# One layer of an attention, recurrence and ConvGLU step: the tail folded into the last pair, and three stages reordered

## The reference

```python
h = rmsnorm(x, g_mix) * (1 + sc1) + sh1
q = (rmsnorm(pq, g_q) @ w_uq).reshape(B, T, 8, 96)      # 64 plain + 32 rotated columns
kv = (ckv_keys @ w_ukv).reshape(B, K, 8, 128)
o_mla = mla_attention(...)                              # 8 heads
o_hg = hgrn2_branch(...)                                # 4 heads
mix = sigmoid(ga) * (o_mla @ w_mla_o) + sigmoid(gb) * (o_hg @ w_hg_o)
x = x + gt1 * (mix @ w_out)
h2 = rmsnorm(x, g_ffn) * (1 + sc2) + sh2
gate, val = split(h2 @ w_ffn_in)
u = gelu(conv3(gate)) * val
x = x + gt2 * (u @ w_ffn_out)
y = rmsnorm(x, g_final)
```

## Time and profile before

| | us |
|---|---|
| three runs | 2227.31, 2230.32, 2235.73 (median 2230.32) |
| the profiled execution, its own time | 2230.21 |
| its span, first to last instruction | 2228.4 |
| TensorE busy | 2112.3 (95%) |
| VectorE busy | 964.8 (43%) |
| GpSimd busy | 785.8 (35%) |
| ScalarE busy | 652.1 (29%) |

### The profile page before, as it was taken

One profiled execution on the slowest core, in us unless ns is written; L12 is line 12 of the kernel. 1 busy time (PEld: TensorE's weight loads), 2 busy tenths in 40 slices (PEclk: granted clock), 3 DMA queues, 4 the chain that ended last, 5 costly groups with the idle time before them and its releaser, 6 DMA issues. The chain is left out here.

```text
span 2228.4 us, 28073 instructions
## 1 busy us (share of the span) xinstructions
PE 2112.3 (95%) x11544; PEld 1944.9 (87%) x11544; DVE 964.8 (43%) x1380; ACT 652.1 (29%) x939; POOL 785.8 (35%) x512
## 2 busy tenths in 40 slices
PE   7499999999999998999989889999999999999995
PEld 2479999999999988788879878999999999999994
DVE  2613535343414217556634357243334333433348
ACT  1333232323213334677652211311211121112120
POOL 0334353525213413445534622422322232223234
PEclk9599999999999999999999999999999999999998
DMA  6355311112221247233347423111111111111113
GB/s 239 113 186 112 41 53 32 53 32 60 63 70 48 90 122 211 73 86 85 87 136 203 156 76 104 57 40 37 57 39 38 39 56 40 39 38 53 43 67 132
DMA packets 191407, 183.96 MB, mean 83 GB/s; under 512 B 55047, under 2 KB 159200, under 8 KB 191280
## 3 DMA queue, kind: packets, MB, share of 16 engines
q1 hardware_dynamic: 189984, 177.44, 26.9%
q0 software_dynamic: 1296, 4.72, 0.6%
HBM read 141.36 MB, written 40.78 MB: 82 GB/s over the span
## 5 line engine op out<-in xcount | busy, mean ns | idle before, releaser
L129 POOL TENSOR_TENSOR s_w_lo<-s_w_raw,s_w_hi 128x1024 fp32r<-128x1024 f32 x86 | 219.9, 2557 | 512.4 <-ACT s_w_hi L124 512.4
L822 PE MATMUL s_psum<-h_hi,s_w_hi 128*128 128x384 f32 x1008 | 345.4, 346 | 24.8 <-POOL h_lo L250 24.8
L2567 PE MATMUL s_ps<-h_hi,s_w_hi 128*128 128x384 f32 x1056 | 353.1, 334 | 0.7 <-ACT gate_pad L2410 0.7
L2567 PE MATMUL s_ps<-h_hi,s_w_lo 128*128 128x384 f32 x1056 | 352.9, 334 | 0.0
L2567 PE MATMUL s_ps<-h_lo,s_w_hi 128*128 128x384 f32 x1056 | 352.8, 334 | 0.0
L822 PE MATMUL s_psum<-h_lo,s_w_hi 128*128 128x384 f32 x1008 | 338.8, 339 | 0.0
L822 PE MATMUL s_psum<-h_hi,s_w_lo 128*128 128x384 f32 x1008 | 338.5, 339 | 0.0
L822 PEld LDWEIGHTS s_psum<-h_hi,s_w_hi 128*128 128x128 f32 x1008 | 191.1, 190 | 34.9 <-issue 19.3
L2567 PEld LDWEIGHTS s_ps<-h_hi,s_w_hi 128*128 128x128 f32 x1056 | 198.2, 188 | 1.4 <-issue 1.0
L2567 PEld LDWEIGHTS s_ps<-h_lo,s_w_hi 128*128 128x128 f32 x1056 | 198.2, 188 | 0.4
L2567 PEld LDWEIGHTS s_ps<-h_hi,s_w_lo 128*128 128x128 f32 x1056 | 198.2, 188 | 0.0
(11 more groups left out here) (365 smaller groups left out, 3848.8 us busy)
## 6 DMA issues: line engine op xcount, KB each, us to landing
s_w_raw<-in_w_ffn_in SPq DMA_DIRECT2D x44, 512.0 KB, 3.7
s_w_raw<-in_w_in SPq DMA_DIRECT2D x41, 512.0 KB, 3.9
s_w_mod<-in_w_mod SPq DMA_DIRECT2D x8, 2048.0 KB, 8.0
w_raw<-in_w_ffn_out SPq DMA_DIRECT2D x11, 1024.0 KB
scratch_gates<-sig SPq DMA_DIRECT2D x48, 192.0 KB, 1.9
merge_gates<-scratch_gates SPq DMA_DIRECT2D x16, 576.0 KB, 3.9
w_mod<-in_w_mod SPq DMA_DIRECT2D x4, 2048.0 KB, 10.4
scratch_o_mla<-o_raw SPq DMA_DIRECT2D x8, 576.0 KB, 4.6
```

What stands on the lines that cost most here:

```text
L129: pool.tensor_tensor(flat[0], flat[1], flat[2], ALU.subtract).then_inc(self.lo_ready, 1)
L822: return pe.matmul(bank(j), wx[c % 2][:, k, :], hx[:, k, j * CH:(j + 1) * CH], start=(k == 0 and n == 0), stop=(k == KD - 1 and n == 2))
L2567: mm = pe.matmul(ps[bank][:, 0:CH], a[s][:, k, :], b[:, k, j * CH:(j + 1) * CH], start=n == 0, stop=n == 3 * KD - 1)
```

## The change

Four places are edited.

1. Attention units: the first head's three query units stand between value units 6 and 7 instead of behind the second k group. H and G of the first head stand behind unit k(1,2) instead of q(2,2), and its tops start behind q(1,0), one for each unit, instead of behind k(2,0). The F sums stand later.
2. Merge: blocks 2 and 3 of the attention rows are divided and split at later chunks (divided at 1, 2, 4, 6, split at 2, 3, 5, 7).
3. Out stage: tile t's transposes stand one by one behind outputs 6, 7, 8, 9, 11, 13, 15 and 17; DVE and ACT follow that order.
4. Tail: `yacc` is multiplied by gt2 (`z_gate`, nine of 128x1024 on DVE) and x1 is added to it (`z_add`, 18 of 128x512 on POOL) ahead of the end, in pairs 9 and 10, tile 8 first. What is left for a tile at the end is: both PSUM halves times gt2, one add of `yacc`, a square and sum that is on ACT now, the root, the reciprocal and the scale. TensorE's order there is the same; its banks are freed by the product with gt2 (`e_gated`) instead of by the sum (`e_sum`). gt2 is loaded twice more, x1 in 18 half rows through four buffers, and `gate_pad`, `conv` and `w2_raw` lie at other addresses to make room.

```diff
-    units = [("k", 0, u) for u in range(3)] + [("v", t, 0) for t in range(10)]
+    units = [("k", 0, u) for u in range(3)] + [("v", t, 0) for t in range(7)]
+    units += [("q", 0, u) for u in range(3)] + [("v", t, 0) for t in range(7, 10)]
     units += [("k", 1, u) for u in range(3)]
-    for h in range(HEADS):
+    for h in range(1, HEADS):
...
+FIRST_TOPS = {unit: n for n, unit in enumerate(B_UNITS[B_AT["q", 1, 0]:][:len(TOP_UNITS)])}
+FIXED_AFTER = {("q", 1, 0): 0, ("q", 1, 1): 1, ("q", 1, 2): 2, ("q", 2, 0): 3, ("q", 2, 1): 4}
...
-                if (kind, x, u) == ("q", 2, 2):
+                if (kind, x, u) == ("k", 1, 2):
                     item("H", 0, 0)
                     item("G", 0, 0)
...
+        X_DIV_AT, X_HI_AT, X_LO_AT = (1, 2, 4, 6), (2, 3, 5, 7), (2, 3, 5, 7)
...
-                    if c - 2 < KB:
-                        split_x(c - 2)
+                    if c in X_HI_AT:
+                        split_x(X_HI_AT.index(c))
...
-                    for ready in {3: (0,), 4: (1, 2), 5: (3,), 6: (4,), 7: (5, 6), 8: (7,)}[t]:
-                        transposes(ready)
+                        if o in TRANSPOSED_AFTER:
+                            transposes(TRANSPOSED_AFTER.index(o))
...
+                    if g == LAST - 1:
+                        sp.dma_start(gt2_once[:, :], io["rows"][3:4, :].to_broadcast([P, D])).then_inc(once_loaded, 16)
+                        for i in range(4):
+                            load_back(i)
...
+                for i in range(4, O_UNITS):
+                    load_back(i)
...
+                    act.wait_ge(e_x2, t + 1)
+                    if t >= 3:
+                        act.wait_ge(e_stored[t % 3], 16 * (t // 3))
+                    act.activation(fin[t % 3][:, :], x2[t % 3][:, :], ACT.Square, accum_out=stat[:, 3, t:t + 1]).then_inc(e_sq, 1)
...
+                def z_add(n):
+                    pool.wait_ge(z_gated, n + 1)
+                    for i in (2 * n, 2 * n + 1):
+                        cols = slice(i % 2 * HALF, (i % 2 + 1) * HALF)
+                        pool.wait_ge(back_loaded[i % 4], 16 * (i // 4 + 1))
+                        z = yacc[:, Z_TILES[n], cols]
+                        pool.tensor_tensor(z, z, x1_back[i % 4][:, :], ALU.add).then_inc(z_ready, 1)
...
+                z_add(0)
+                z_add(1)
+                w.split_lo(pool, 0, 4 * LAST + 2)
+                for t in range(2, 5):
+                    z_add(t)
+                w.split_lo(pool, 1, 4 * LAST + 3)
+                z_add(5)
+                z_add(6)
+                u_split(LAST, 0)
+                w2_split(LAST)
+                u_split(LAST, 1)
+                z_add(7)
+                z_add(8)
-                for t in range(TILES):
-                    pool.wait_ge(e_gated, t + 1)
-                    pool.wait_ge(back_loaded[t % 3], 16 * (t // 3 + 1))
-                    pool.tensor_tensor(x2[t % 3][:, :], yacc[:, t, :], x1_back[t % 3][:, :], ALU.add).then_inc(e_x2, 1)
...
-                        pe.wait_ge(e_sum, o - 7)
+                        pe.wait_ge(e_gated, o - 7)
...
+                    if g == LAST - 1:
+                        z_gate(0)
+                    if g == LAST:
+                        for n in range(5, TILES):
+                            z_gate(n)
                     conv_gate(g, 1)
                     value(g, 0)
                     value(g, 1)
+                    if g == LAST - 1:
+                        for n in range(1, 5):
+                            z_gate(n)
...
-                        dve.tensor_tensor(dst, dst, ps[(6 + o) % 8][:, :], ALU.add).then_inc(e_sum, 1)
-                    dve.wait_ge(e_sum, 2 * t + 2)
-                    dve.tensor_tensor(yacc[:, t, :], yacc[:, t, :], gt2[group(t)][:, :], ALU.mult).then_inc(e_gated, 1)
+                        dve.tensor_tensor(x2[t % 3][:, cols], ps[(6 + o) % 8][:, :], gt2[group(t)][:, cols], ALU.mult).then_inc(e_gated, 1)
...
-                    dve.tensor_tensor_reduce(fin[t % 3][:, :], x2[t % 3][:, :], x2[t % 3][:, :], 1.0, 0.0,
-                                             ALU.mult, ALU.add, stat[:, 3, t:t + 1]).then_inc(e_sq, 1)
...
                 for t in range(TILES):
-                    end_sums(t)
+                    end_gate(t)
+                    dve.wait_ge(e_gated, 2 * t + 2)
+                    dve.wait_ge(z_ready, O_UNITS)
+                    dve.tensor_tensor(x2[t % 3][:, :], x2[t % 3][:, :], yacc[:, t, :], ALU.add).then_inc(e_x2, 1)
                     if t >= 1:
-                        end_square(t - 1)
                         end_scale(t - 1)
```

More of the change, by code:

```diff
@@ L1371 @@
 TOP_UNITS = tuple(("M", u) for u in range(16)) + (("P", 0), ("P", 1), ("C", 0), ("T", 0))
-def first_tops():
-    out, n = {}, 0
-    for unit in B_UNITS[B_AT["k", 2, 0]:]:
-        take = 2 if unit[0] == "k" and unit[1] == 3 and unit[2] < 2 else 1
-        if n < len(TOP_UNITS):
-            out[unit] = range(n, min(n + take, len(TOP_UNITS)))
-        n += take
-    return out
-FIRST_TOPS = first_tops()
-FIXED_AFTER = {("q", 0, 1): (0,), ("q", 0, 2): (1,), ("q", 1, 0): (2,), ("q", 1, 1): (3,), ("q", 1, 2): (4,)}
+FIRST_TOPS = {unit: n for n, unit in enumerate(B_UNITS[B_AT["q", 1, 0]:][:len(TOP_UNITS)])}
+FIXED_AFTER = {("q", 1, 0): 0, ("q", 1, 1): 1, ("q", 1, 2): 2, ("q", 2, 0): 3, ("q", 2, 1): 4}
 HEAD_ITEMS = (
@@ L1598, in walk @@
                 unit(kind, x, u)
-                for n in FIXED_AFTER.get((kind, x, u), ()):
-                    item("F", n, 0)
+                if (kind, x, u) in FIXED_AFTER:
+                    item("F", FIXED_AFTER[kind, x, u], 0)
                 if (kind, x, u) == ("q", 0, 2):
@@ L2210 @@
 O_UNITS = 2 * TILES
+TRANSPOSED_AFTER = (6, 7, 8, 9, 11, 13, 15, 17)
 def flat_pieces(j):
@@ L2253, in stage_out_ffn @@
         yacc = late("yacc", [P, TILES, D])
-        over = Arena(nc, home.top)
+        over = Arena(nc, first.at)
         g_base = over.at
@@ L2258, in stage_out_ffn @@
         w2_raw = over("w2_raw", [P, 2, D])
-        assert over.at <= HIGH
+        gt2_once = over("gt2_once", [P, D])
+        x1_back = [over("x1_back3", [P, HALF])]
+        assert over.at <= HIGH - 8
         w2_hi, w2_lo = late("w2_hi", [P, 2, D], F32R), late("w2_lo", [P, 2, D], F32R)
         u_hi, u_lo = late("u_hi", [P, 2, NT], F32R), late("u_lo", [P, 2, NT], F32R)
+        x1_back = [late(f"x1_back{i}", [P, HALF]) for i in range(3)] + x1_back
         assert late.at <= first_end
@@ L2277, in stage_out_ffn @@
         gfin = end("g_final_row", [P, D])
-        x1_back = [end(f"x1_back{i}", [P, D]) for i in range(3)]
         x2 = [end(f"x2_{i}", [P, D]) for i in range(3)]
@@ L2295, in stage_out_ffn @@
         y_ps, y_added = sems("y_product"), sems("y_added")
-        end_rows, back_loaded = sems("end_rows"), [sems(f"back_loaded{i}") for i in range(3)]
-        e_ps, e_sum, e_gated, e_x2 = sems("end_product"), sems("end_sum"), sems("end_gated"), sems("end_x2")
+        end_rows, once_loaded, back_loaded = sems("end_rows"), sems("once_loaded"), [sems(f"back_loaded{i}") for i in range(4)]
+        z_gated, z_ready = sems("z_gated"), sems("z_ready")
+        e_ps, e_gated, e_x2 = sems("end_product"), sems("end_gated"), sems("end_x2")
         e_sq, e_std, e_rstd = sems("end_sq"), sems("end_std"), sems("end_rstd")
@@ L2306, in stage_out_ffn @@
         Y_PAIRS = PAIRS - 2
+        Z_TILES = (TILES - 1,) + tuple(range(TILES - 1))
         with nc.Block() as block:
@@ L2330, in load_w2, with load_back @@
                     sp.dma_start(w2_raw[:, :, :], wout[:, 2 * g:2 * g + 2, :]).then_inc(w2_loaded, 16)
+                def load_back(i):
+                    t, half = Z_TILES[i // 2], i % 2
+                    if i >= 4:
+                        sp.wait_ge(z_ready, i - 3)
+                    sp.dma_start(x1_back[i % 4][:, :], io["x1"][t * P:(t + 1) * P, half * HALF:(half + 1) * HALF]
+                                 ).then_inc(back_loaded[i % 4], 16)
                 load_wo(4)
@@ L2440, in _ @@
                 std(1)
-                std(2)
                 h_split(0)
-                std(3)
-                h_split(1)
-                h_split(2)
-                for t in range(4, TILES):
+                for t in range(2, TILES):
                     std(t)
@@ L2520, in _ @@
                 w.split_lo(pool, 0, 2)
-                for g in range(PAIRS):
+                def z_add(n):
[5 more added lines that the diff above has]
+                        pool.tensor_tensor(z, z, x1_back[i % 4][:, :], ALU.add).then_inc(z_ready, 1)
+                for g in range(LAST):
                     if g > 0:
@@ L2746, in _ @@
                 residual(1)
-                residual(2)
                 affine(0)
-                residual(3)
-                affine(1)
-                affine(2)
-                for t in range(4, TILES):
+                for t in range(2, TILES):
                     residual(t)
```

69 lines of the change are left out of this document (30 added, 39 removed).

## The result

| | before | changed |
|---|---|---|
| runs shown with the result, median | 2229.82 us (2227.31 to 2235.73) | 2198.72 us (2197.92 to 2200.13) |
| the profiled execution, its own time | 2230.21 | 2197.92 |
| its span | 2228.4 | 2196.1 |

The ratio is 0.985, with a 95% interval of 0.9835 to 0.9864 (the two medians of the table alone give 0.986): 31.1 us less by the medians, 32.3 by the two profiled executions. A second set of runs of the changed kernel gave 2198.58 (ratio 0.9853, 0.9839 to 0.9866). The forecast was 2205.6, 24.6 less, with a range of 2196 to 2215. The time lies in it, near its lower end. From group to group the kernel before had medians of 2229.8 to 2231.4, and the changed kernel 2198.7 and 2198.6; within a group the runs of the changed kernel lie up to 2.4 us apart.

The account below looks back on a forecast made before the run. TensorE bounds the kernel up to its last products, DVE the tail. Tail −13.7 (−16.9 and +3.2 in the last pair), out stage −6.6, units −2, merge −2.3: −24.6 on 2230.21 gives 2205.6 us, range 2196 to 2215.

Parts of the forecast that it names:

- The tail: End of the kernel: TensorE sets the pace instead of DVE, with 5.0 us behind its last product; −16.9 us.
- The last pair: Before the tail: moved adds and products on POOL and DVE run end to end, so TensorE waits; +3.2 us.
- no stall in the last pair: Rival: both engines' work fits in before 2141.03, DVE having been idle 12.45 us earlier; −3.2, 2202.4 us, chance 0.16.
- The next margin: Last pair: splits of u and w2 end at about 2156, TensorE arrives at 2156.7; no second stall, under 1 us spare.
- The out stage: Reordered transposes, residuals and affines: waits for `h_y` and slow transposes of 9.6 us shrink to 3.0; −6.6 us.
- The units: Attention units: `q_hi` wait stays or grows to 7.6, row-of-maxima wait goes, sequence ends earlier; −2 us.
- The merge: Merge: a weight's ACT copy no longer queues behind the last quotient's, so the 3.0 us lo-part stall shrinks; −2.3 us.
- The stall that I let remain: Merge: the weight's lo part comes at 1190.2, while TensorE wants it at 1189.5.
- The rival on the other side: Slower: the last pair's stall drops TensorE's clock to 0.50 through the tail; up to 2254 us, chance 0.04.

Follow-up runs that it names:

- two experiments: Changed kernel with x1's 18 half-row adds on DVE: 2207.31 us; changed kernel with four more gt2 products between pair 10's two conv_gates: 2205.63 us.

## Why the prediction was right, and where its sum was off

**The tail** was right: −16.9 forecast for its length, −16.5 measured, with TensorE setting the pace and a chain of 5.0 us behind it. By that sum DVE had 1.4 us to spare a tile; in the run with the square on DVE nothing is to spare, and 3.7 us are lost, most of them (2.9) behind the last product.

**The last pair** is the term that failed: "Together 27.5, to 2144.2", +3.2. It was +0.1. The engines do hinder each other as the earlier trace rows show, but laid end to end the work of both was 4 us too long (27.5 against 23.5). Some 0.7 of it was done before `conv_gate(10,0)` began, since the third half add had started. The rest is overlap in every pair of instructions: an alternating product and half add take 2.1 to 2.26, not 1.23 + 1.29 = 2.52, which is 1.0 for four products, and the two taps beside a half add and a lo part took 5.82, not 2 × 1.42 + 1.29 + 2.40 = 6.53. The rule of the Trainium skill (SBUF — State Buffer, "SBUF: two separate sides") stands in so far as DVE slows from 1.23 to over 2 us, yet the sum of full durations overstated the stretch here. The rival "no stall in the last pair" (2202.4) is what happened, mainly for this reason and not for the idle time ahead that it named. That the margin was under 1 us fits with four products more, which cost 6.9. The next margin came as forecast: the last split of w2 ended at 2136.77, 1.0 us before TensorE's first output product. The whole lies 6.9 us below the forecast: 3.1 are of this term, 2.6 of the units and heads, and up to 3.5 are not of the change at all; the out stage missed by 1.3 the other way, and that these partly cancel is luck.

**The out stage**: −6.6 forecast, −5.3 by the traces and 6.5 by undoing it. Two waits are left, 0.43 and 2.40, where 3.0 were forecast.

**The units**: −2 forecast; the traces give −3.6 and another −1.0 in the heads, undoing it 7.6, of which the lengths of the stages show 5.3 and 2. The term can be redone from the point at which `q_hi` releases the first tops. That point came 10.1 us earlier, counted from the end of the projection stage (52.1, then 42.0), where 9.5 were forecast. TensorE's work behind it grew by 9.1, where 9 were forecast, and the wait ahead of it to 7.75 as worked out. What was mis-sized are the waits behind it: from 4.0 us to 1.3. The prediction had the row of maxima and the last unit (2.7 became 1.3); the two waits for `att_tops` (0.5 and 0.8), which also went, it put at nothing. The waits at the value units (0.7 and 1.4 before, for ACT and DVE, which wait for their stores) lie ahead of the release by `q_hi` and are covered by it.

The heads were put at 0. Windows at the first scores, in the kernel before and in the changed one (columns as in the earlier trace rows):

```profile
900.50:904.50 4.00, 3.97 (x11) 3.21 (x12) 0.00 (x0) 1.55 (x2) 0.00 (x0) 0.60 0.37 111
893.40:897.40 4.00, 4.00 (x17) 3.14 (x18) 0.13 (x1) 2.51 (x4) 1.01 (x1) 1.00 0.37 111
```

Behind the wait of 2.7 us for the row of maxima TensorE was granted 0.60 and did 11 matmuls where it did 17 behind the wait of 1.3. The run with the old units shows 0.60 too, behind 2.8 us, and has a wait of 0.9 more in a later head; the run with tops four later shows 0.50 and then 0.73, behind 2.8. It does not follow every time: with tops five later, behind 2.5 us, it was 1.00. So in the kernel before the removed wait cost itself and about 1 us of the heads.

**The merge**: −2.3 forecast and −2.3 between the traces, 1.2 to 2.0 by undoing it. The stall that I let remain (0.7) comes in some executions, with 0.9 to 2.2 us.

**The clock.** The rival on the other side can be judged: two experiments have a stall shortly before the tail. Windows of the kernel with the adds on DVE (columns as in the earlier trace rows):

```profile
2129.00:2133.00 4.00, 2.23 (x7) 2.26 (x8) 2.61 (x5) 2.42 (x3) 0.02 (x1) 0.50 0.00 0
2133.00:2137.00 4.00, 4.00 (x21) 4.00 (x20) 0.00 (x0) 0.00 (x0) 4.00 (x3) 0.81 0.00 0
2145.23:2194.70 49.47, 49.45 (x216) 40.18 (x215) 30.87 (x41) 14.01 (x27) 2.77 (x2) 1.00 0.27 107
```

After 5.2 us without work TensorE ran at 0.50, the level of 1.2 GHz, then rose again, and the tail took the same 49.47 us as in the changed kernel. With 5.2 and 4.7 us of waits the two experiments lost 7.1 and 6.7 us in ConvGLU: a stall costs itself and about 2 us, not the stage behind it. The shares that this rival named were also off: from 2205.6 to the bound of 2219.2 are 13.6 us, over a quarter of a tail of 49 and not a fifth, and to 2241.5 are 35.9, nearly three quarters and not half.

**Not of the change.** 3.5 of the 32.3 us between the first two traces lie in the projection stage, whose code is the same. It ended at 803.1 to 805.2 in eight profiled executions and at 806.2 to 808.1 in six, the kernel before among the latter. In the first pair the granted clock from 120 to 140 us was 0.92 before and 1.00 after. A single pair of traces overstates the change by that much.
